# Five more full-precision spare products between the weight products of a two-block transformer kernel

## What is computed

```python
def first_block(...):
    xn = rms_norm(h, norm1_g)
    proj = einsum(xn, w_in)                 # feeds four branches y_a .. y_d
    merged = sum(sigmoid(xn @ w_gate[n] + b_gate[n]) * (y[n] @ w_branch[n]) for n in range(4))
    h = h + merged @ w_out
    hn = rms_norm(h, norm2_g)
    h = h + square(relu(hn @ w_ff1)) @ w_ff2
    h = h + sigmoid(rms_norm(h, norm3_g) @ w_ple_gate + b_ple_gate) * (p @ w_ple)
    return rms_norm(h, final_g)

def second_block(...):
    h = modulate(rms_norm_2(x, norm1_g), sh1, sc1)
    z = h @ w_in + b_in                     # feeds the mLSTM (ym) and the attention (ya)
    merged = sigmoid(ga) * (ym @ p_mlstm) + sigmoid(gb) * (ya @ p_moba)
    x = x + g1 * (merged @ w_out)
    h = modulate(rms_norm_2(x, norm2_g), sh2, sc2)
    x = x + g2 * ((silu(h @ w_gate) * (h @ w_up)) @ w_down)
    return rms_norm_2(x, normf_g)
```

## Time and profile before

| what | value |
|---|---|
| median of 3 runs | 908.36 us (907.76 to 909.52) |
| span of the profiled execution, first to last instruction | 906.8 us |
| time of the profiled execution beside its span | not listed; the median is 1.5 us above the span |
| TensorE busy | 894.0 us, 99% of the span, 7,368 records |
| VectorE busy | 732.1 us, 81% |
| ScalarE busy | 569.8 us, 63% |
| share of the DMA engines | 63%, 209 GB/s in the mean |

### The profile page before, as it was taken

The page is one execution under the profiler, slowest core; times in us unless marked ns, Lnnn a source line. Parts: engine busy times, 40 slices in busy tenths (PEclk is TensorE's granted clock), DMA queues, the critical chain, the costliest instruction groups (busy, mean ns, idle before and its releaser), DMA issues.

```text
span 906.8 us, 18499 instructions
## 1 busy us (share of the span) xinstructions
PE 894.0 (99%) x7368; PEld 869.1 (96%) x7368; DVE 732.1 (81%) x1164; ACT 569.8 (63%) x830; POOL 1.9 (0%) x9
## 2 busy tenths in 40 slices
PE   9999999999999999999999999999999999999996
PEld 7999989999999999999999999899999999999996
DVE  6778998899998899898966999988688975555454
ACT  7848456775586787664446868677776754444541
POOL 0000000000000000000000000000000000000000
PEclk9999999999999999999999999999999999999999
DMA  8766555566875789988865566744455566565541
GB/s 319 252 189 228 149 161 180 163 186 206 282 259 164 268 288 349 354 315 312 331 191 167 174 219 202 191 154 138 143 167 182 163 210 186 186 186 186 188 139 47
DMA packets 53157, 189.83 MB, mean 209 GB/s; under 512 B 6208, under 2 KB 6864, under 8 KB 52944
## 3 DMA queue, kind: packets, MB, share of 16 engines
q1 hardware_dynamic: 52928, 188.65, 63.0%
q10 hardware_dynamic: 144, 0.00, 0.0%
HBM read 186.53 MB, written 1.05 MB: 207 GB/s over the span
## 4 chain that ended last, share of the span: by engine, by line
PE 87%; DVE 6%; ACT 5%; issue 1%; DMA 1%; SPq 0%; ACTq 0%; DVEq 0%
PE bank L1014 25%; PE bank L1016 25%; PE bank L1017 25%; PE bank L987 2%; PE bank L989 2%; PE bank L988 2%; DVE wlo L1053 1%; ACT whi L1886 1%; ACT gates L2331 1%; DMA H<-in_xT 1%; PE bank L722 1%; DVE hsc L1549 1%; PE bank L663 0%; PE bank L959 0%; ACT L2331 0%
## 5 line engine op out<-in xcount | busy, mean ns | idle before, releaser
L1053 DVE TENSOR_TENSOR wlo<-raw,whi 128x1024 fp32r<-128x1024 f32 x297 | 361.0, 1222 | 98.1 <-ACT whi L1886 96.9
L1886 ACT ACTIVATE whi<-raw 128x1024 fp32r<-128x1024 f32 x297 | 312.0, 1057 | 201.5 <-PE bank L1017 188.4
L1014 PE MATMUL bank<-Alo,whi 128*128 128x256 f32 x1344 | 377.9, 281 | 0.0
L1016 PE MATMUL bank<-Ahi,wlo 128*128 128x256 f32 x1344 | 373.7, 278 | 0.0
L1017 PE MATMUL bank<-Ahi,whi 128*128 128x256 f32 x1344 | 373.7, 278 | 0.0
L1014 PEld LDWEIGHTS bank<-Alo,whi 128*128 128x128 f32 x1344 | 254.0, 189 | 2.9 <-issue 2.6
L1016 PEld LDWEIGHTS bank<-Ahi,wlo 128*128 128x128 f32 x1344 | 252.7, 188 | 0.4 <-issue 0.2
L1017 PEld LDWEIGHTS bank<-Ahi,whi 128*128 128x128 f32 x1344 | 252.6, 188 | 0.0
L1016 PE MATMUL bank<-Fhi,wlo 128*128 128x256 f32 (+1 forms) x320 | 88.8, 278 | 0.0
L1017 PE MATMUL bank<-Fhi,whi 128*128 128x256 f32 (+1 forms) x320 | 88.8, 278 | 0.0
L1014 PE MATMUL bank<-Flo,whi 128*128 128x256 f32 x256 | 70.9, 277 | 0.0
(11 more groups left out here) (407 smaller groups left out, 1382.2 us busy)
## 6 DMA issues: line engine op xcount, KB each, us to landing
raw<-in_stream SPq DMA_DIRECT2D x298, 512.0 KB, 4.3
araw<-in_ada SPq DMA_DIRECT2D x48, 512.0 KB, 5.9
TB<-in_TB SPq DMA_DIRECT2D x1, 1536.0 KB, 6.8
a8r<-a SPq DMA_DIRECT2D x16, 64.0 KB, 4.0
bc<-in_bc SPq DMA_DIRECT2D x1, 896.0 KB, 6.1
out<-H SPq DMA_DIRECT2D x3, 256.0 KB, 2.2
H<-in_xT SPq DMA_DIRECT2D x1, 512.0 KB, 7.3
mats<-in_mats SPq DMA_DIRECT2D x1, 449.0 KB, 7.1
```

The costliest lines, as they stand in the source:

```text
L1014: pe.matmul(os[j], wh, xl, start=k == 0 and (wide or j == 0), stop=False, skip_group_check=not wide)
L1016: pe.matmul(os[j], wl, xh, start=False, stop=False, skip_group_check=not wide)
L1053: v.tensor_tensor(wlo[:, s % NHL, :], raw[:, s % NRAW, :], whi[:, s % NHL, :].bitcast(F32), ALU.subtract).then_inc(*lo_v.up(s))
L1886: a.activation(whi[:, s % NHL, :], raw[:, s % NRAW, :], ACT.Copy).then_inc(*hi.up(s))
```

## The change

Five entries are added to the table of spare products. No other line is touched.

```diff
@@ -175,7 +175,7 @@
 
 ROPE = (0, 2, 1, 3)
 
-BETWEEN = {40: 3, 68: 7, 183: 5}
+BETWEEN = {40: 3, 68: 7, 90: 5, 183: 5, 226: 6, 238: 7, 241: 7, 246: 7}
 STEPS = {
     "r1": ([3], [4], [3, 5]),
     "xa": ([], [5, 6, 7, 8, 9], [5, 6, 7, 8]),
```

## The result

The changed kernel took 909.01 us (median of 20 runs) against 903.29 us for the kernel before (median of 20 runs); the ratio of the undisturbed runs is 1.0058, with a 95% interval from 1.0042 to 1.0074. It is slower by 0.6%, where 0.7% faster was forecast. Two of the 20 runs of the changed kernel were disturbed (1,270 and 1,805 us) and count in neither the ratio nor what follows; the other 18 have a median of 908.96 us: 904.1 and 904.3 us, and sixteen between 907.4 and 910.6.

A forecast was written before the change was run, and what follows sets the result against it. TensorE bounds the kernel: number of products times the time from one to the next, plus few waits. Terms of -0.62, -0.30 and -5.56 sum to -6.5 us, from a median of 908.36 to 901.9 us; 8-in-10 range 900.8 to 904.6 us.

The forecast's parts named there:

- the cost of 0.23 us a product: On TensorE: each spare product takes 0.46 us where two ordinary intervals would take 0.23 to 0.24; five cost 1.15 us.
- the supply of weights carries the fast pace to the end: Last stretch: VectorE and DMA have room for the faster pace; the tight place, behind slab 90, has 0.86 us in hand.
- nothing comes between after 724.62 us, and the slow pace holds to the end: Last stretch: no interruption between products, so the pace of 117.8 ns, against 113.4 ns elsewhere, lasts to 896.81 us.
- the term for the last stretch: Slabs 238, 241 and 246: 1,416 products turned fast gain 6.25 us, less 0.69 for three spare products: -5.56 us.
- a single short one mostly sets it fast: TensorE's stream: one short call without a wait is followed by the fast pace, in seven of eight cases ahead of 256-column products.
- The terms of slabs 90 and 226: In w_out of the first and second block: 192 and 120 products turned fast, less 0.23 us each: -0.62 and -0.30 us.
- A: Rival: spare products don't turn the last stretch; 908.1 us with slabs 90 and 226 working, 909.5 with none; chance 0.16.
- C: Rival: slab 90's shift spoils ff1 and ff2, up to 1,536 products slow, 6.8 us, at most 916.3 us; chance 0.04.
- B: Rival: only part of the change works, or TensorE meets a wait; 0.5 to 2.5 us less gain, 902.4 to 904.4; chance 0.20.
- whatever ran before: The skill's one gap, 109 ns for 256 columns, taken as independent of history; by it the change costs +1.15 us.

## Why the prediction was wrong

**The count over all 13 traces.** The plain product alone, straight between two products of 256 columns, with no wait: from F to S17 21 times in 21, from S17 to F 11 in 11, from S14 to S17 5 in 5, from S16 to S17 4 in 4. From the 258-column products it gave F 13 times in 13. So P is followed by the slow pace from every state of the 256-column stream but S17. Of the 39 bare waits of these traces (at about 283, 689 and 724 us) 14 left F, 11 S14, 9 S16 and 5 S17.

**Right.** The two paces, 113.4 and 117.8 ns, and that an interruption decides which one follows; the granted clock of 1.00 in both; the cost of 0.23 us a product; and that the supply of weights carries the fast pace to the end (149 us at 113 ns without a wait, in the kernel without 246). No late weight turned up: the changed kernel's trace has the same three bare waits. The 258-column stretches with their sum didn't change either, 12.03 us against 12.00. Slab 90 worked in the profiled execution, but by luck: its wait at 283 us happened to leave S17, the one state from which P gives F.

**The first step that failed** is "nothing comes between after 724.62 us, and the slow pace holds to the end", taken as a property of the kernel. It holds for one execution. The wait at 724 us left, in 13 traces, F four times, S14 five times, S16 twice and S17 twice, and with F the last 1,462 products were fast without any help. I had three times, all from the slow group, and one profile, and made the whole sum against 908.36 us; the kernel before has a median of 903.29 us in 20 runs. Of the 5.56 us that the term for the last stretch promised, fifteen of those 20 had nothing to give, and so had half of all 101.

**The second** is "a single short one mostly sets it fast", from seven of eight. The eight were of different kinds. Three were sums of 256 columns and one of 512 (L587, L606, L671), which begin from F but for one from S14, and from S17 left S17 in three traces; one stood behind the 258-column products, one behind the heads' products and two behind 512-column products. Not one was the case of the change: P alone behind products of 256 columns. The nearest to it, the two sums in a row of L760, was against it: those gave S17 from F in all 13 traces. What the row at 617.87 us showed was taken for a matter of the moment, and was the same in every trace.

**What took their place.** With three products behind the last wait, F, S14 and S16 end in S17, and only S17 ends in F. From the 13 draws that is S17 at the end 11 times in 13; measured were sixteen of 18 runs above 907 us. Where the wait leaves F, which costs the kernel before nothing, the change adds 1,224 slow products (5.4 us) and some 72 between 238 and 241 (0.3), and three products, 0.7 us: 6.4 us, where the prediction had -5.56.

The terms of slabs 90 and 226, -0.62 and -0.30, failed by the same step: behind 226 the profiled execution went from S14 to S17 and stayed slow, and the two early products alone measured +1.3 to +1.4 us and not -0.92. (By the table, the one at 90 adds 1.3 us where the wait at 283 us left S14 or S16 and 2.1 where it left F, and gives back 1.7 only from S17.) Together that is 7.8 us against runs of before that were fast in the last stretch; from the median of its eight fastest, 900.6 us, to the 909.0 of the change it is 8.3. The 5.7 us between the two medians are less, since before has its own five above 907 us and the group near 903.3 us. In the two profiled executions nothing of this shows in the span (906.8 and 906.5 us), since the one of before was slow all through the last stretch: it would have been read as a small success.

**The rivals.** A, the last stretch isn't turned, named 909.5 us with none of the five working, with a chance of 0.16. The measured 909.01 is near that by luck: the new products did act, turning the last stretch three times, and A's sum starts from a median of 908.36 us that more runs don't bear out. C put the loss into ff1 and ff2, of which only the 240 products behind slab 98 came true, in three of the four traces with one plain product at slab 90, and not in that of the change. B had a later product that turns a fast stretch back, but for 72 to 192 products. What no rival had is that the last of three does it, for 1,224 products, and that the stretch can be fast without the change. The Trainium skill (TensorE: Matmul & The Clock Gate, "Back-to-back issue gap") gives N / 2.4 + 2.5 ns, 109 ns for 256 columns, for a product by itself, and says there that in a stream of weight loads and products both set the distance. So the prediction, with its "whatever ran before", held that figure against a case for which the page doesn't give it. The traces show 113.4 and 117.8 ns here, never 109.

## What to carry to other kernels

Where the same instructions run at two rates in one trace, the state is part of the measurement: look at what each wait leaves in several traces before you cost an edit against one of them, and take more than three times. Sort the evidence by the exact kind of interruption and by the state it starts from; a count over unlike cases gave seven of eight here, and the like cases gave none of 21 from F and none of 9 from S14 and S16. If you use spare work to set such a state, use a form that ends in the wanted state from all of them (two plain products in a row did from F, S17 and S14, a transpose and a product from F and S17; from S16 neither was caught in a trace, though all 12 runs of each were fast), once, behind the last wait.

## What the runs showed of the hardware

The stream of load and product pairs has one steady state at the fast pace and three at the slow one, at a granted clock of 1.00, 113.4 and 117.8 ns a pair; a slow one shows one load in three at 192 ns instead of 188, always on the same place of the period of three. A 128-column full-precision product between them maps these states in a fixed way, 41 times in 41 (F, S14 and S16 to S17, S17 to F); two in a row (four records) gave F 7 times in 7, from F, S17 and S14. Why the hardware has these states, and which part of it the loads meet at 192 ns, stays open; so does a group of the kernel before near 903.3 us (seven of its first 20 runs), 2 to 3 us above its fastest, which no trace here has caught. An estimate from the table fits its place but isn't shown: if the wait at 283 us leaves S17 (slow to slab 108, 468 products) and the one at 689 us S14, S16 or S17 (168), that is 636 products by 4.4 ns, 2.8 us.
